# Gate tiles of a recurrent layer: the four tiles of few rows behind the six full ones

## The reference

```python
u = rmsnorm(x, norm_g) @ w_in
xb, gate = u[..., :1536], u[..., 1536:]
xb = causal_depthwise_conv(xb, conv_w, conv_b)          # 4 taps
xs = xb.reshape(bsz, seq, 16, 96)                       # 16 blocks of 96 channels
r = sigmoid(einsum('bshi,hij->bshj', xs, wr) + br)      # block-diagonal, 96 x 96
i = sigmoid(einsum('bshi,hij->bshj', xs, wi) + bi)
a = exp(-8 * r * softplus(-lam))
b = sqrt(1 - a * a) * (i * xb)
hs = associative_scan(a, b)                             # h[t] = a[t] h[t-1] + b[t]
x = x + (hs * silu(gate)) @ w_out
```

## Time and profile before

| | |
|---|---|
| median of 3 runs | 1131.48 us (1131.18 to 1131.64) |
| span of the profiled execution, first to last instruction | 1129.3 us |
| what lies around the span, median less span | 2.2 us |
| PE busy | 1118.0 us, 99% |
| DVE, ACT, POOL busy | 642.8 us, 519.2 us, 160.9 us |
| mean granted clock of PE | 0.998 |
| gates of group 1, 2, 3, 4 begin on PE | 40.85, 81.99, 127.68, 173.94 us |

### The profile page before, as it was taken

One profiled execution on the slowest core, in us unless ns is written; L12 is line 12 of the kernel. 1 busy time (PEld: TensorE's weight loads), 2 busy tenths in 40 slices (PEclk: granted clock), 3 DMA queues, 4 the chain that ended last, 5 costly groups with the idle time before them and its releaser, 6 DMA issues.

```text
span 1129.3 us, 14393 instructions
## 1 busy us (share of the span) xinstructions
PE 1118.0 (99%) x5336; PEld 886.7 (79%) x5336; DVE 642.8 (57%) x1093; ACT 519.2 (46%) x909; POOL 160.9 (14%) x198
## 2 busy tenths in 40 slices
PE   9999999999999999999999999999999999999997
PEld 6787787887677788767778888888888888888886
DVE  7787977887668674465454545555443333544232
ACT  6656567465666544244344433335433212333131
POOL 2022111320323221022121200021000000000021
PEclk9999999999999999999999999999999999999999
DMA  6322323332111123211322122223223232223212
GB/s 227 113 75 93 97 90 100 106 111 86 55 48 68 57 93 103 93 57 56 113 75 94 68 82 95 102 84 112 93 93 112 79 108 93 94 95 111 93 57 75
DMA packets 31270, 103.28 MB, mean 91 GB/s; under 512 B 3552, under 2 KB 5984, under 8 KB 31200
## 3 DMA queue, kind: packets, MB, share of 16 engines
q1 hardware_dynamic: 30624, 101.74, 26.4%
q10 hardware_dynamic: 576, 0.62, 0.2%
HBM read 99.72 MB, written 2.10 MB: 90 GB/s over the span
## 4 chain that ended last, share of the span: by engine, by line
PE 88%; DVE 6%; ACT 4%; issue 2%; DMA 1%; SPq 0%; POOL 0%; DVEq 0%; ACTq 0%; POOLq 0%
PE ps L754 26%; PE ps L756 25%; PE ps L755 25%; PE ps L877 3%; PE ps L892 3%; PE ps L923 2%; DVE wl L1262 2%; DVE xs L1341 1%; PE ps L917 1%; DVE sg L1357 1%; DVE cc L1373 1%; DMA xt<-xT 1%; ACT wh L956 1%; ACT aa L1031 0%; ACT cc L1044 0%
## 5 line engine op out<-in xcount | busy, mean ns | idle before, releaser
L754 PE MATMUL ps<-xgh,wh 128*128 128x512 f32 x847 | 336.7, 398 | 1.2 <-issue 0.7
L756 PE MATMUL ps<-xgh,wl 128*128 128x512 f32 x847 | 330.2, 390 | 0.0
L755 PE MATMUL ps<-xgl,wh 128*128 128x512 f32 x847 | 329.9, 390 | 0.0
L1262 DVE TENSOR_TENSOR wl<-raw,wh 128x1024 fp32r<-128x1024 f32 x180 | 230.9, 1284 | 137.8 <-ACT wh L956 137.4
L956 ACT ACTIVATE wh<-raw 128x1024 fp32r<-128x1024 f32 x180 | 188.4, 1049 | 127.7 <-PE ps L756 127.1
L754 PEld LDWEIGHTS ps<-xgh,wh 128*128 128x128 f32 x847 | 159.1, 188 | 39.0 <-issue 6.7
L756 PEld LDWEIGHTS ps<-xgh,wl 128*128 128x128 f32 x847 | 159.0, 188 | 33.8
L755 PEld LDWEIGHTS ps<-xgl,wh 128*128 128x128 f32 x847 | 159.2, 188 | 32.5 <-issue 1.0
L1738 POOL TENSOR_SCALAR Pt<-Pt,stat 128x256 f32<-128x256 f32 (+2 forms) x128 | 75.1, 599 | 274.0 <-DVE stat L1519 198.9
L754 PE MATMUL ps<-fh,wh 128*128 128x512 f32 x240 | 93.4, 389 | 0.0
L755 PE MATMUL ps<-fl,wh 128*128 128x512 f32 x240 | 93.4, 389 | 0.0
(11 more groups left out here) (232 smaller groups left out, 1579.0 us busy)
## 6 DMA issues: line engine op xcount, KB each, us to landing
raw<-wst SPq DMA_DIRECT2D x180, 512.0 KB, 3.5
bst<-nbias SPq DMA_DIRECT2D x8, 256.0 KB, 3.4
xt<-xT SPq DMA_DIRECT2D x3, 512.0 KB, 7.6
outT<-ot SPq DMA_DIRECT2D x2, 384.0 KB, 2.5
outT<-ot SPq DMA_DIRECT2D x6, 128.0 KB, 2.0
cstt<-cst SPq DMA_DIRECT2D x1, 448.0 KB, 5.3
raw<-wst SPq DMA_DIRECT2D x1, 320.0 KB, 4.6
xt<-xT ACTq DMA_DIRECT2D x1, 256.0 KB, 3.4
```

The costliest lines, as they stand in the source:

```text
L754: e.matmul(o, high, a, start=(k == 0), stop=False)
L755: e.matmul(o, high, b, start=False, stop=False)
L756: e.matmul(o, low, a, start=False, stop=stop).then_inc(tile_done, 1)
L1262: e.tensor_tensor(wl_t[:, u % NHL, :], raw_t[:, u % NRAW, :], f32(wh_t[:, u % NHL, :]), ALU.subtract).then_inc(lo_done, 1)
```

## The change

Within each group the four over tiles are moved behind the six full tiles, in the order 2, 0, 3, 1:

gr c, gi c, gr c+1, gr c+2, gi c+1, gi c+2, over 2, over 0, over 3, over 1

The banks are taken in the same order as before. The end of gr c and gi c is now the ninth tile (before: the seventh), the end of gr c+1 and gr c+2 the eighth (before: the sixth), the end of gi c+1 and gi c+2 the tenth as before. `at_over`, the index of over 2, becomes the seventh tile. The due times of the gates of all three chunks are 2 ticks later than they were, and with them those of the roots and scans of group 4. The weight stream is reordered to match; its length is the same.

```diff
--- before.py
+++ after.py
@@ -99,15 +99,17 @@
 
 
         c = 3 * g
-        for own, over in (([("gr", c), ("gi", c)], 2), ([("gr", c + 1), ("gr", c + 2)], 0), ([], 3), ([("gi", c + 1), ("gi", c + 2)], 1)):
-            for name in own:
-                self.take(name)
-                self.tiles.append((name, 0, False))
-            if over == 2:
-                self.at_over[g] = len(self.tiles)
+        for name in [("gr", c), ("gi", c), ("gr", c + 1), ("gr", c + 2), ("gi", c + 1), ("gi", c + 2)]:
+            self.take(name)
+            self.tiles.append((name, 0, False))
+        self.at_over[g] = len(self.tiles)
+        for over in (2, 0, 3, 1):
             self.tiles.append((("over", g, over), 1, False))
-            for name in own or [("gr", c), ("gi", c)]:
-                self.end[name] = len(self.tiles) - 1
+            if over == 3:
+                self.end["gr", c] = self.end["gi", c] = len(self.tiles) - 1
+            if over < 2:
+                for m in (c + 1, c + 2):
+                    self.end[("gr", "gi")[over], m] = len(self.tiles) - 1
         for m in range(c, c + 3):
             for kind in ("gr", "gi"):
                 self.n_act += 1
@@ -553,7 +555,7 @@
         SUMS = {1: "wa", 2: "wb", 3: "wc"}
 
         def gate_tick(c):
-            return end["gi", c] + 1.2 + 3.5 * (c % 3 > 1)
+            return end["gi", c] + 1.2 + (0.0, 2.0, 5.5)[c % 3]
 
         def root_tick(g):
 
@@ -1810,14 +1812,12 @@
         for n in range(2):
             over[n, 96:128] = full[n, g, 96:128, 128:256]
             over[n, 0:32] = full[1 - n, g, 256:288, 128:256]
-        add(over[:1])
         for n in range(2):
             f = full[n, g]
             add(f[None, 0:128, 0:128])
             add(f[None, 256:384, 256:384])
-            add(np.concatenate([f[128:192, 0:128], f[192:256, 256:384]])[None])
-            if n == 0:
-                add(over[1:])
+        halves = [np.concatenate([f[128:192, 0:128], f[192:256, 256:384]]) for f in full[:, g]]
+        add(np.stack([over[0], halves[0], over[1], halves[1]]))
     add(wo[:2, 6:9])
     add(wo[2:6, :9])
     add(wo[:6, 9:])
```

## The result

The changed kernel takes 1135.38 us (median of 6 runs, 1133.66 to 1136.67) against 1131.35 us (6 runs, 1131.18 to 1131.64). The ratio is 1.0034, interval 1.0023 to 1.0046: slower, by more than the 1.8 us forecast and outside its range. The scatter has grown: the six runs before lie within 0.5 us (1.3 us in the 31 runs of it beside the first experiments), those after within 3 us. It goes with the granted clock of the run: the one run of six at 0.998 took 1133.66 us, the others, at 0.994 or 0.995, took 1134.86 to 1136.67. The profiled execution is one of these (1135.79 us, 1.8 us around its span; the 2.2 us given for the kernel before set the median against the span of another run).

A forecast was written before the change was run, and what follows sets the result against it. PE, 99% busy, was taken as the bound, but stopped where it meets DVE's output. The silu 11 read-out swallows the switch gain up to there and leaves PE 1.79 us late: 1131.48 + 1.79 = 1133.3 us, range 1131.3 to 1134.3.

The forecast's parts named there:

- (a): PE's gate tiles, every group: row-shape switches fall from 7 to 5, saving 0.41 us per group, 1.65 us in four.
- the wait of over 3 for over 2: Gate tiles on PE: one tile of 0.89 us between them instead of three; costed at nothing, upper bound 0.3 us.
- a wait that the forecast said would not be there: PE behind the gates: the changed profile would show no wait for yl, the low half of a recurrence output.
- (b): Sixth gate tile, group 3: PE waits for DVE's silu 8 read-out until 133.75, standing still 2.5 us start to start.
- The wait of group 4: Sixth gate tile, group 4: could start at 178.5, but PE waits for DVE's silu 11 read-out until 180.0.
- (c): DVE and ACT chain: first tanh moves from 46.85 to 48.02; silu 11 read-out ends up 0.11 us late, bounds 0 and 1.2.
- the border swap: Borders of groups 2/3 and 3/4: split done before c2 saves 1.41 us against 0.95 for the split, giving 0.46 back.
- Rival C: First gate starts 1.17 us late on ACT, border gives no 0.46 back: 1133.8 to 1134.4 us; 20 in 100.
- a sign of being wrong: DVE's silu read-outs, groups 3 and 4: the forecast is wrong if they move by more than 0.5 us.
- B: Gate gains lost at yl waits, bank wait hidden: no change, 1131.5 us, from 1131.1 to 1132.1; 14 in 100.
- rival D: Behind the 2.5 us stop PE's clock falls to half, 3 us for 15 matmuls: 1136 us; 2 in 100.
- the 1.79 us of the stop: PE in group 4, tile behind the yl tile: starts at 186.60 instead of 184.81, set by DVE's silu 11 read-out.

The follow-up runs named there:

- first run: The changed kernel with the old tile order in groups 3 and 4, changed due times in all four groups: 1131.01 us, ratio 0.9994.
- the stop in group 4: The changed kernel with the old tile order in group 3 only, new order in groups 1, 2 and 4, changed due times: 1137.03 us, ratio 1.005.
- the run with the short stop: The changed kernel with DVE's split of weight units 22 and 30 moved behind the last silu read-out of groups 3 and 4: 1132.34 us, ratio 1.0007.

## Why the prediction was wrong

**(a) The switches**: right. Five per group, 0.2 us each; the four over tiles of group 1 take from 45.16 to 48.73, 3.57 us, as the forecast of 4 x 0.89, so the wait of over 3 for over 2, put at nothing, cost nothing. The ten tiles of group 1 take 7.84 us (40.89 to 48.73), 0.49 less than before, where the forecast had 0.41. And, as forecast, nothing of it reached the end. It is given back at a wait that the forecast said would not be there, for yl at 92.06: PE takes that tile 0.4 us later than before.

**(b) The bank wait**: right in place, cause and size: PE stops ahead of the sixth gate tile of group 3 until 133.60 (forecast 133.75). The wait of group 4, forecast until 180.0, did not come, because PE arrived later than the read-out.

**(c) The chain of DVE and ACT**: right to 0.1 us until the clock fell, and the run with due times alone shows the border swap by itself. Rival C (the border swap gives nothing back) is refuted. Behind the fall the chain is late with PE: silu 11 is read out at 181.23, 2.2 us later than before, and the forecast had named 0.5 us as a sign of being wrong.

The lower end of the range was called B's middle; B went from 1131.1 to 1132.1, so its middle is 1131.6 and not 1131.3, and nothing hangs on it.

**The step that failed is the weighing of rival D**, the fall of the clock behind the stop. It had its place and its direction, and 2 chances in 100, on the ground that no earlier stop was as long. That ground does not bear on it: a trace without a stop as long says nothing of what such a stop does. So the sum had a term of nothing for the clock, and it comes in 9 of 10 runs. Rival D's own size was off as well, in the length of the stretch: 3 us for 15 steps at half clock, where the profile has 21 (12 of few rows, 9 of wa) from 134.49 to 144.74. They take 10.25 us, and 5.74 by the forecast's steps, so each step loses 0.21 us, as D had it. The first tile of conv 9 starts at 144.74; the forecast's 139.66 for the tile before it, plus 0.69, gives 140.35. So 4.4 us are lost there, and still at the fourth gates (179.52, forecast 175.1). The stop in group 4, forecast with 1.5 us (178.5 to 180.0), is then spared; at the tile behind the yl tiles the difference is 189.45 - 186.60 = 2.85 us. With the 1.79 us of the stop that is 4.64 us over the earlier trace rows, and the span grew by 4.7 (1134.0 - 1129.3). That rival D's 1136 lies near the measured 1135.4 and 1136.1 is thus in part luck: it took too short a stretch, and it left out the stop in group 4 that the fall spares. The forecast of 1133.3 is near the time of the one run of this kernel at full clock, 1133.66.

The page "TensorE: Matmul & The Clock Gate" of the Trainium skill ("Part 1: The HAM clock gate") says that the share of clock pulses that PE gets takes only the values of half and full; the windows of 0.50 between windows of 1.00 agree.

What is shown: the order in groups 3 and 4 makes the stop (first run); a stop of 2.6 us from start to start lowers the clock with full tiles behind it as well (nine of ten); with the few-row tiles behind it, half clock lasts longer (10.2 us in four profiles: the changed kernel twice, the old due times, the stop in group 4; against 6.9 us, 5.3 of them behind the stop, in the one profile with full tiles that caught a fall). The mean clocks agree: 13 of the 17 runs of the first kind with a fall are at 0.994 and four at 0.995, and none of the 14 of the second kind (nine with a stop of 2.65 us, five with 3.74 us) is under 0.995. What is open: why four few-row tiles hold the clock down. They have few rows and they have switches, and no run took the one without the other. The stops ahead of full tiles also stood at another place, behind the gates and not in them. Stops between 1.75 and 2.65 us were not tried. Nor was the changed order in groups 3 and 4 with no wait at all: all six banks of the ring are used by the gates, and the last full tile must take the newest.

## What to carry to other kernels

Before you move a tile forward in a queue, look up whose buffer it takes and when that is read out; an engine that is 99% busy may still have only 0.7 us of slack there. A stop of the matmul engine has a second price, the clock behind it: weigh it by what the clock costs for some 3 to 10 us (0.2 us for each step of 0.23 in it), not by whether an earlier trace shows a fall. And split a change into its order and its due times: here the due times alone gain 1.4 us, and the order that leaves the last tile in place keeps it.

## What was not expected of the hardware

The clock fell behind stops of 2.65 to 2.69 us in nearly all runs (nine of ten with full tiles; nine of ten, four of four and four of four with few-row tiles), behind 3.74 us in five of five, behind 1.75 us in one of ten and behind 1.55 us with full tiles in none of ten. Behind a stop of 1.51 us with two few-row tiles it never did; behind 1.17 us with four it did in five of ten runs, counting the kernel's two places together. Nor does it fall in step with the stop: in the profiles it fell 1.6 us before PE went on (full tiles) and 0.5 to 1.3 us after (few-row tiles), and in the run with the short stop 2.6 us after. The same stretch of four with nothing stopped ahead of it ran at full clock, at 183.69 in the changed kernel and in all ten runs of the first experiment.
